# A two-block sequence model in float32 on one core: two re-orderings, in the opening norm and after the last expert

## The chip, the cores and the metric

The program runs on one core of one Trainium2 chip. The metric is the device time of one execution in microseconds; it was measured three times. The core has a matrix engine (TensorE, in the profile PE, with its weight loads as PEld), a vector engine (VectorE, DVE), a scalar engine (ScalarE, ACT), GpSimd (POOL, not used here) and SyncE (SP), whose queue issues all the transfers. The engines run on their own and meet only at semaphores. SBUF is the on-chip memory of 128 partitions; PSUM has eight banks of 512 float32 columns, which TensorE writes.

## The reference

`x` is 512 tokens by 1024. Block 1 is a norm, a projection, two mixers (a gated spatial mixer, and a state space model called S5 here), a merge with a residual, then 16 experts, each of which takes the 64 tokens that score best for it. Block 2 is a norm, a gated recurrence beside a retention, and a convolved FFN. Everything is float32.

```python
h = rms_norm(x, norm1_g[l])
p = h @ w_in[l]
...
gate, idx = lax.top_k(scores, cap)                       # 16 experts, 64 tokens each
a = jnp.einsum('becd,edf->becf', xs, w_gate)
u = jnp.einsum('becd,edf->becf', xs, w_up)
y = jnp.einsum('becf,efd->becd', jax.nn.silu(a) * u, w_down)
y = (y * gate[..., None]).astype(h.dtype)
out = jax.ops.segment_sum(y.reshape(-1, dm), seg, num_segments=bn * seq)
...
return rms_norm(x, final_g)                              # end of block 1, start of block 2
```

## The kernel before

Outside the experts a product of float32 values is made of three products of a faster type (fp32r). A weight chunk of 1 MB lands in `raw`; ScalarE rounds it into `hi` (`make_hi`, line 408), VectorE takes the rest, `lo = raw - hi` (`make_lo`, line 417); the activations are split in the same way into `xh` and `xl`, in eight tiles of 128 x 512 (tile k holds features 128k to 128k+127 of all tokens). TensorE adds hi by xh, hi by xl and lo by xh (line 471). The experts' products are plain float32. The order of work on each engine is the order in which the code is written, since each takes its instructions in turn. Chunks are numbered; `hi_done`, `lo_done` and `pe_used` count those rounded, subtracted and used up.

**Opening.** `first_act` and `first_dve` split x (`x_hi`, line 748, and `rest`, line 904), with `x_in0` to `x_in2` telling that tiles 0-1, 2-3 and 4-7 have landed. Chunk 0 has 256 columns and is used tile by tile (lines 635 to 637), so TensorE waits for `xl` of each tile. Between these splits stand small operations for the S5 tables in `TY` (16 columns each): two Sin on ScalarE (lines 763, 764), whose function table must be loaded first, and after them, on VectorE, products of `TY` (lines 921 to 931), the start values `BB` and `BF`, and powers `PW`, `PT`, `PD` (to line 959). Then `inputs(q)` and `outputs(q)`, for four quarters q, make `V` and `CL` by six wide operations each (lines 873 to 881), which TensorE takes in `tables(q)` (lines 608, 620). The squares of x (`sq`, line 514) are summed on TensorE (line 531), ScalarE takes the root (line 549), VectorE the reciprocal (line 991, `rb_done`), and TensorE spreads it (`spread_first`: lines 542 and 646) in the middle of chunk 1, after output tile 1 of 4 of its hi pass. `take` (line 987) multiplies a pair of chunks' result in PSUM by the spread `rb`; its `qq_taken` frees PSUM for the next pair.

**Experts.** A stream of 192 chunks of 2 MB (`load_x`), 12 for each expert, runs through a ring of eight buffers `xs`: eight chunks of gate and up weights (line 1231) and four of down weights (`down`, line 1243). A down chunk holds 512 of the 2048 rows of `w_down` by all 1024 columns, so the output `ps[:, YB]` is complete only after the fourth. Its matmuls have 64 columns of weights (64 tokens in `hidT`) and write one half of the partitions each: columns 0 to 511 of the result to partitions 0 to 63, the others to 64 to 127. ScalarE then copies the result times the gate value into `yy` (line 1350), TensorE spreads `yy` over the tokens with the one-hot matrix `t1` (`scatter`, line 588, eight matmuls, one for each tile of x), and VectorE adds each to `xt` (`take_scattered`, line 1420). Experts go in pairs, and the scatter of a pair stands in the next pair; that of the last pair stands behind everything.

**Start of block 2.** ScalarE makes `xh` (line 1698) and two squares (line 1700) of each tile of `xt`, VectorE `xl` (line 1466). The first chunk of block 2 (`NEXP`, which is 21) is used tile by tile; the sums of the squares (line 1485) follow it, then chunk 22. Its buffers `hi[0]` and `lo[0]` lie where `xs[2]` lay.

## Time and profile before

| | us |
|---|---|
| median of three runs | 1861.78 (1859.52 to 1862.80) |
| profiled execution, its own time | 1860.12 |
| its span | 1858.4 |
| PE busy | 1714.5 (92%) |
| DVE busy / ACT busy | 658.4 / 445.4 |
| DMA moved | 492.52 MB |

The profiled execution's own time is 1.7 us above its span and 1.7 us below the median of the three runs. Times in the rows are counted from the start of the span. PE busy is not PE at its peak, since matmuls overlap; an idle time is shown in brackets with what ended it. The granted clock is given as a share of full speed: 1.00 is 2.4 GHz, 0.50 is 1.2 GHz.

### The profile page before, as it was taken

The numbers are of one execution on the slowest core, as the hardware profiler recorded it, in microseconds if no ns is written. First come the engines' busy times: TensorE is split into PE (matmuls) and PEld (weight loads), VectorE is DVE, ScalarE is ACT, GpSimd is POOL, SyncE is SP. The second block draws the span as 40 slices with busy tenths as digits, with TensorE's granted clock in tenths as the row PEclk, the third lists the DMA queues.
The fourth block names the chain that finished last, engine by engine and source line by source line (L and its number), as shares of the span: only waits on it lengthen the run. The fifth ranks groups of instructions, "written<-read, shape, count | busy, mean of one in ns | idle before, by whom it ended". The sixth has DMA issues, their size and how long they took to land. (4 is left out here: it accounts for less than half of the span.)

```text
span 1858.4 us, 20146 instructions
## 1 busy us (share of the span) xinstructions
PE 1714.5 (92%) x8461; PEld 1036.3 (56%) x8461; DVE 658.4 (35%) x916; ACT 445.4 (24%) x555; POOL 0.2 (0%) x4
## 2 busy tenths in 40 slices
PE   6999996999897997988979889789999999999998
PEld 5888883343242432424324243247778888888886
DVE  8786533101010010100101001047645565645745
ACT  5434322110010100101001010055433433423333
POOL 0000000000000000000000000000000000000000
PEclk9999998999999999999999999999999999999999
DMA  6234437999999999999999999952412223222311
GB/s 201 69 104 160 164 146 278 409 428 428 427 428 427 428 429 429 428 428 428 428 428 429 428 428 428 428 207 89 158 67 70 91 91 113 90 92 90 113 46 45
DMA packets 74920, 492.52 MB, mean 265 GB/s; under 512 B 7408, under 2 KB 11504, under 8 KB 49904
## 3 DMA queue, kind: packets, MB, share of 16 engines
q1 hardware_dynamic: 74864, 491.71, 65.5%
q8 instruction: 43, 0.70, 0.2%
q14 instruction: 13, 0.11, 0.0%
HBM read 487.49 MB, written 2.10 MB: 263 GB/s over the span
## 5 line engine op out<-in xcount | busy, mean ns | idle before, releaser
L1231 PE MATMUL ps<-xs,xe 128*64 128x512 f32 x2048 | 462.9, 600 | 66.0 <-DMA xs<-w_up 33.1
L1231 PEld LDWEIGHTS ps<-xs,xe 128*64 128x64 f32 x2048 | 142.2, 137 | 379.5 <-issue 265.8
L1243 PE MATMUL ps<-xs,hidT 128*64 128x512 f32 x1024 | 229.7, 596 | 14.1 <-DMA xs<-w_down 9.9
L417 DVE TENSOR_TENSOR lo<-raw,hi 128x2048 fp32r<-128x2048 f32 x72 | 162.6, 2259 | 170.2 <-ACT hi L408 167.2
L1452 DVE TENSOR_TENSOR hid<-hid,ps 128x512 f32<-128x512 f32 x32 | 20.6, 684 | 525.9 <-PE ps L1231 525.9
L408 ACT ACTIVATE hi<-raw 128x2048 fp32r<-128x2048 f32 x72 | 136.0, 1889 | 204.5 <-PE ps L447 93.9
L471 PE MATMUL ps<-xh,hi 128*128 128x512 f32 x416 | 164.9, 396 | 0.9 <-DVE ga L987 0.9
L471 PE MATMUL ps<-xl,hi 128*128 128x512 f32 x416 | 162.3, 390 | 0.0
L1243 PEld LDWEIGHTS ps<-xs,hidT 128*64 128x64 f32 x1024 | 73.7, 137 | 148.3 <-issue 120.5
L447 PE MATMUL ps<-xh,hi 128*128 128x512 f32 x384 | 150.2, 391 | 1.4 <-DVE xt L2013 1.1
L447 PE MATMUL ps<-xl,hi 128*128 128x512 f32 x384 | 149.4, 389 | 0.0
L471 PE MATMUL ps<-xh,lo 128*128 128x512 f32 x416 | 102.1, 390 | 0.0
L447 PE MATMUL ps<-xh,lo 128*128 128x512 f32 x384 | 90.9, 389 | 0.0
L471 PEld LDWEIGHTS ps<-xh,hi 128*128 128x128 f32 x416 | 78.1, 188 | 20.0 <-issue 2.6
L471 PEld LDWEIGHTS ps<-xl,hi 128*128 128x128 f32 x416 | 78.1, 188 | 15.9 <-issue 0.2
L471 PEld LDWEIGHTS ps<-xh,lo 128*128 128x128 f32 x416 | 77.8, 188 | 16.2
L1338 ACT ACTIVATE hidT<-ps 128x512 f32<-128x512 f32 x32 | 18.6, 597 | 281.5 <-PE ps L1271 281.5
L447 PEld LDWEIGHTS ps<-xh,hi 128*128 128x128 f32 x384 | 72.0, 188 | 18.1 <-issue 3.0
L1420 DVE TENSOR_TENSOR xt<-xt,ps 128x512 f32<-128x512 f32 x64 | 44.0, 688 | 107.6 <-PE ps L588 107.6
L1335 ACT ACTIVATE hid<-ps 128x512 f32<-128x512 f32 x32 | 17.4, 594 | 267.2 <-PE ps L1231 267.1
L447 PEld LDWEIGHTS ps<-xl,hi 128*128 128x128 f32 x384 | 72.1, 188 | 15.1 <-issue 0.2
L447 PEld LDWEIGHTS ps<-xh,lo 128*128 128x128 f32 x384 | 72.1, 188 | 15.0
(432 smaller groups left out, 1747.5 us busy)
## 6 DMA issues: line engine op xcount, KB each, us to landing
xs<-w_up SPq DMA_DIRECT2D x64, 2048.0 KB, 32.8
xs<-w_gate SPq DMA_DIRECT2D x64, 2048.0 KB, 31.9
xs<-w_down SPq DMA_DIRECT2D x64, 2048.0 KB, 31.4
raw<-w_in SPq DMA_DIRECT2D x24, 1024.0 KB, 7.7
raw<-ffn_up_w SPq DMA_DIRECT2D x24, 1024.0 KB, 5.1
raw<-ffn_down_w SPq DMA_DIRECT2D x12, 1024.0 KB, 5.1
raw<-w_out SPq DMA_DIRECT2D x8, 1024.0 KB, 5.1
raw<-w_up_a SPq DMA_DIRECT2D x2, 1024.0 KB, 7.6
```

What stands on the lines that cost most here:

```text
L408: act.activation(hi[slot][:, 0:size], raw[:, raw_slot(n), 0:size], ACT.Copy).then_inc(sem("hi_done"), 1)
L417: dve.tensor_tensor(lo[slot][:, 0:size], raw[:, raw_slot(n), 0:size], hi[slot][:, 0:size].bitcast(F32), ALU.subtract).then_inc(sem("lo_don ...
L447: mm = pe.matmul(ps[:, bank + m, 0:nn if token_major else SEQ], l, r, start=(k == 0 and part == 0 and q == 0), stop=(last and part == 1 an ...
L471: mm = pe.matmul(ps[:, bank + m, :], l, r, start=(opens and kk == 0 and part == 0 and q == 0), stop=(closes and part == 1 and kk == nk - 1))
L1231: mm = pe.matmul(ps[64 * half:64 * half + 64, bank + b, :], xe[:, k, CAP * u:CAP * (u + 1)], xs[n % NXS][:, f:f + 512], start=(k == 0), st ...
L1243: mm = pe.matmul(ps[64 * nn:64 * nn + 64, YB, :], hidT[:, 4 * (c % 2) + kk, CAP * half:CAP * (half + 1)], xs[n % NXS][:, kk * D + nn * 512 ...
L1335: a(hid[:, 512 * b:512 * b + 512], ps[:, GB + b, :], ACT.Silu).then_inc(sem("sil_done"), 1)
L1338: a(hidT[:, 4 * b:4 * b + 4, :].rearrange("p k c -> p (k c)"), ps[:, TB + b, :], ACT.Copy) \
L1420: tt(xt[:, m, :], xt[:, m, :], ps[:, TB + m % 3, :], ALU.add).then_inc(sem("sc_taken"), 1)
L1452: tt(hid[:, 512 * b:512 * b + 512], hid[:, 512 * b:512 * b + 512], ps[:, UB + b, :], ALU.mult) \
```

## The change

There are two parts.

In the opening, ScalarE makes `xh` of tiles 4 to 7 before the two Sin, VectorE makes `xl` of tiles 4 to 7 before the products of `TY`, and the reciprocal moves ahead of chunk 1's `make_lo` and of `inputs(0)`.

After the experts, the last expert's down weights arrive in another cut: chunk q holds all 2048 rows of columns 256q to 256q+255, from a copy `w_down_q` that the host lays out, so a quarter of the result is complete after each chunk. Chunk q takes 32 matmuls of 128 columns in place of 8 of 512. The third quarter lies in the second halves of `xs[6]` and `xs[7]`, the fourth in `xq3`, over space that the gathered tokens used; The space of `xh` and `xl` of tiles 0 to 3 (the first halves of the same two buffers) is not used by these chunks. SyncE issues the third quarter after 184 used chunks and not 183. After each quarter ScalarE evicts two pieces of 64 x 128, and TensorE scatters the two tiles of the quarter before; VectorE adds tiles 0 to 5 before chunk 21's `make_lo` and tiles 6 and 7 after it.

```diff
@@ first_act
             x_hi(range(2, 4))
+            x_hi(range(4, KD))
             a(TY[:, 10, :], TY[:, 6, :], ACT.Sin).then_inc(sem("exp_done"), 1)
             a(TY[:, 11, :], TY[:, 7, :], ACT.Sin).then_inc(sem("exp_done"), 1)
-            x_hi(range(4, KD))
@@ first_dve
-            for k in range(2, 4):
+            for k in range(2, KD):
                 rest(k)
...
+            dve.wait_ge(sem("nrm_rms"), 1)
+            dve.reciprocal(rs[0], rs[0]).then_inc(sem("rb_done"), 1)
             make_lo(dve, 1)
...
             inputs(0)
-            dve.wait_ge(sem("nrm_rms"), 1)
-            dve.reciprocal(rs[0], rs[0]).then_inc(sem("rb_done"), 1)
             make_lo(dve, 2)
@@ experts_pe
+            def down_by_columns(i):
+
+                pe.wait_ge(sem("hidT_done"), i * 4 + 4)
+                for q in range(4):
+                    n = NX - 4 + q
+                    x_arrived(pe, n, 0)
+                    if q >= 2:
+                        pe.wait_ge(sem("yy_done"), YLAST + 2 * (q - 1))
+                    home = last_home[q]
+                    for c in range(4):
+                        for kk in range(4):
+                            f = 256 * (4 * c + kk)
+                            for nn in range(2):
...
+                                mm = pe.matmul(ps[64 * nn:64 * nn + 64, last_bank(q), 0:P],
+                                               hidT[:, 4 * (c % 2) + kk, CAP * (c // 2):CAP * (c // 2 + 1)], wv,
+                                               start=(c == 0 and kk == 0), stop=(c == 3 and kk == 3))
+                    mm.then_inc(sem("xs_used"), 1)
+                    if q:
+                        last_scatter(q - 1)
+                last_scatter(3)
+
+            def last_scatter(q):
+
+                if q == 0:
+                    pe.wait_ge(sem("t1_done"), NE // 2 + 1)
+                pe.wait_ge(sem("yy_done"), YLAST + 2 * (q + 1))
+                for m in (2 * q, 2 * q + 1):
+                    if m >= 2:
+                        pe.wait_ge(sem("sc_taken"), KD * (NE // 2) + min(m, 6))
+                    pe.matmul(ps[:, scatter_bank(m), :], yy[:, m * P:(m + 1) * P], t1[:], start=True, stop=True) \
+                        .then_inc(sem("sc_ps"), 1)
@@ experts_act
-                        act.wait_ge(sem("xs_used"), NX - 4)
+                        for q in range(4):
+                            act.wait_ge(sem("xs_used"), NX - 3 + q)
+                            for nn in range(2):
+                                o = 64 * nn
+                                a(yy[64:P, 256 * q + 128 * nn:256 * q + 128 * nn + 128], ps[o:o + 64, last_bank(q), 0:P], ACT.Copy,
+                                  scale=cur[o:o + 64, 1, 1:2]).then_inc(sem("yy_done"), 1)
+                            if 1 <= q < 3:
+                                new_tile(act, 2 * q - 2)
+                                new_tile(act, 2 * q - 1)
                         make_hi(act, NEXP)
+                        break
@@ experts_dve
-            make_lo(dve, NEXP)
...
+            for m in range(4):
+                add_last(m)
+                if m % 2:
+                    new_rest(m - 1)
+                    new_rest(m)
+            for m in range(4, KD):
+                if m == 6:
+                    make_lo(dve, NEXP)
+                add_last(m)
+            for m in range(4, KD):
+                new_rest(m)
             make_lo(dve, NEXP + 1)
@@ second_act (new_tile is the old loop's body: xh and two squares)
+            for m in range(4, KD):
+                new_tile(act, m)
+                if m == 5:
                     make_hi(act, NEXP + 1)
@@ sync
+            for q in range(4):
+                n = NX - 4 + q
+                sp.wait_ge(sem("xs_used"), min(n - NXS + 1, NX - NXS) if q < 2 else NX - NXS)
+                src = w["w_down_q"][:, q, :]
+                d(last_home[q], src.rearrange("p (a b) -> p a b", a=2) if q == 2 else src).then_inc(x_sem(n % NXS), 16)
```

On VectorE, the place of the reciprocal. `lo_54` is chunk 1's rest, `V` is made by `inputs(0)`, `sm` is the norm's reciprocal. Before:

```order
L958 COPY PD<-PW 64x256
L959 COPY PD<-PW 64x256
L417 TENSOR_TENSOR lo_54<-raw,hi_51 128x2048
L873 TENSOR_TENSOR V_67<-PD,BB 128x512
L874 TENSOR_TENSOR TMP<-PD,BB 128x512
L875 TENSOR_TENSOR V_67<-PD,BB 128x512
L876 TENSOR_TENSOR TMP<-PD,BB 128x512
L877 TENSOR_TENSOR V_67<-V_67,TMP 128x512
L881 TENSOR_TENSOR V_67<-V_67,TMP 128x512
L991 RECIPROCAL sm<-sm 128x128
```

And in the changed kernel, where the same lines have numbers higher by 3 to 5:

```order
L961 COPY PD<-PW 64x256
L962 COPY PD<-PW 64x256
L964 RECIPROCAL sm<-sm 128x128
L422 TENSOR_TENSOR lo_54<-raw,hi_51 128x2048
L878 TENSOR_TENSOR V_67<-PD,BB 128x512
L879 TENSOR_TENSOR TMP<-PD,BB 128x512
L880 TENSOR_TENSOR V_67<-PD,BB 128x512
L881 TENSOR_TENSOR TMP<-PD,BB 128x512
L882 TENSOR_TENSOR V_67<-V_67,TMP 128x512
L886 TENSOR_TENSOR V_67<-V_67,TMP 128x512
L422 TENSOR_TENSOR lo_53<-raw,hi_50 128x2048
```

The reciprocal now stands in front of seven operations that it stood behind.

On ScalarE, the place of the Sin table. Before:

```order
L748 ACTIVATE xh<-xin,prm 128x512 x2
L763 ACT_TABLE_LOAD
L763 ACTIVATE TY<-TY 128x16
L764 ACTIVATE TY<-TY 128x16
L748 ACTIVATE xh<-xin,prm 128x512 x4
L514 ACTIVATE sq<-xin 128x512 x8
```

Now:

```order
L753 ACTIVATE xh<-xin,prm 128x512 x6
L769 ACT_TABLE_LOAD
L769 ACTIVATE TY<-TY 128x16
L770 ACTIVATE TY<-TY 128x16
L519 ACTIVATE sq<-xin 128x512 x8
```

The four `xh` operations moved in front of the table load and the two Sin.

On TensorE, the last expert's down chunks, the scatter (`t_135` is the one-hot matrix) and the first matmul of block 2. Before:

```order
L1243 MATMUL ps<-xs_140,hidT 64x512 x8
L1243 MATMUL ps<-xs_141,hidT 64x512 x8
L1243 MATMUL ps<-xs_142,hidT 64x512 x8
L1243 MATMUL ps<-xs_143,hidT 64x512 x8
L588 MATMUL ps<-t_135,yy 128x512 x8
L471 MATMUL ps<-xh,hi_50 128x512
```

Now:

```order
L1317 MATMUL ps<-xs_140,hidT 64x128 x32
L1317 MATMUL ps<-xs_141,hidT 64x128 x32
L1333 MATMUL ps<-t_135,yy 128x512 x2
L1317 MATMUL ps<-x_144,hidT 64x128 x32
L1333 MATMUL ps<-t_135,yy 128x512 x2
L1317 MATMUL ps<-xq_145,hidT 64x128 x32
L1333 MATMUL ps<-t_135,yy 128x512 x4
L476 MATMUL ps<-xh,hi_50 128x512
```

Each quarter has 32 matmuls where a chunk had 8, and the scatter's eight stand two, two and four.

## Rows read from the trace of the kernel before

**Rows 1.** Windows by stage: PE, PEld, DVE, ACT, POOL busy, clock, DMA share, GB/s.
```profile
340.00:1222.00 882.00, 789.45 (x3640) 297.51 (x3636) 73.94 (x140) 72.91 (x148) 0.00 (x0) 1.00 1.01 428
...
1236.00:1376.00 140.00, 138.16 (x639) 107.42 (x638) 90.08 (x85) 67.59 (x71) 0.00 (x0) 1.00 0.27 96
```

**Rows 2.** Timeline of TensorE: start, us, what; its waits in the first stage.
```profile
17.40 0.36 PE L635 MATMUL ps<-hi,xh 128*128 128x256 f32 x1 [0.77 <-DVE xl L904]
...
34.97 0.81 PE L542 MATMUL ps<-sm 32*128 32x128 f32 x8 [5.80 <-DVE sm L991]
...
139.57 0.50 PE L471 MATMUL ps<-xh,hi 128*128 128x512 f32 x1 [0.85 <-DVE ga L987]
```

**Rows 3.** Busy time by stretch around the wait at 29 us; clock after POOL.
```profile
29.10:35.00 5.90, 0.10 (x5) 0.03 (x4) 5.83 (x9) 0.00 (x0) 0.00 (x0) 0.81 0.54 178
35.00:39.60 4.60, 4.60 (x18) 3.60 (x19) 4.60 (x5) 2.12 (x6) 0.00 (x0) 0.50 0.27 60
```

**Rows 4.** Timeline of VectorE, 14 to 36 us.
```profile
14.39 0.18 DVE L921 TENSOR_TENSOR TY<-TY 128x16 f32<-128x16 f32 x1 [0.83 <-ACT TY L764]
...
19.31 1.05 DVE L940 MEMSET BF<- 128x528 f32 x2
...
27.90 2.29 DVE L417 TENSOR_TENSOR lo<-raw,hi 128x2048 fp32r<-128x2048 f32 x1
...
33.96 0.95 DVE L991 RECIPROCAL sm<-sm 128x128 f32<-128x128 f32 x1
```

**Rows 5.** Timeline of ScalarE, 12 to 17 us.
```profile
12.75 1.28 ACT L763 ACT_TABLE_LOAD   x1
...
14.27 2.55 ACT L748 ACTIVATE xh<-xin,prm 128x512 fp32r<-128x512 f32 x4
16.72 4.26 ACT L514 ACTIVATE sq<-xin 128x512 f32<-128x512 f32 x8
```

**Rows 6.** Issue of x's last four tiles on SyncE's queue.
```profile
3.07 0.83 SPq L2169 DMA_DIRECT2D xin<-x_t  x1
```

**Rows 7.** DMA issues, 0 to 80 us: count, KB, us to landing.
```profile
xin<-x_t SPq DMA_DIRECT2D x1, 1024.0 KB, 10.9
```

**Rows 8.** Timeline of VectorE: its waits before table products and gates.
```profile
56.92 0.69 DVE L873 TENSOR_TENSOR V<-PD,BB 128x512 f32<-128x512 f32 x1 [4.98 <-PE ps L608]
...
83.75 2.48 DVE L987 TENSOR_TENSOR ga<-ps,rb 128x512 f32<-128x512 f32 x4 [1.81 <-PE ps L471]
```

**Rows 9.** Timeline of TensorE: last expert's down products, first chunk.
```profile
1207.78 3.65 PE L1243 MATMUL ps<-xs,hidT 128*64 128x512 f32 x16
```

**Rows 10.** Timeline of TensorE: third and fourth chunk.
```profile
1216.54 3.65 PE L1243 MATMUL ps<-xs,hidT 128*64 128x512 f32 x16 [1.15 <-DMA xs<-w_down]
...
1222.17 3.65 PE L1243 MATMUL ps<-xs,hidT 128*64 128x512 f32 x16 [1.98 <-DMA xs<-w_down]
```

**Rows 11.** Source line 701: 64 instructions of 128x64 weights by 128 columns.
```profile
L701 PEld LDWEIGHTS ps<-wsT,vg x64: 137/137/137, 166.7 to 170.4; 128*64 128x64 f32 x64
L701 PE MATMUL ps<-wsT,vg x64: 272/272/273, 166.8 to 170.5; 128*64 128x128 f32 x64
```

**Rows 12.** Timeline after the last down chunk, all engines.
```profile
1224.93 1.91 ACT L408 ACTIVATE hi<-raw 128x2048 fp32r<-128x2048 f32 x1 [16.65 <-DMA raw<-w_in]
1226.87 1.39 ACT L1350 ACTIVATE yy<-ps,cur 64x512 f32<-64x512 f32 x2
...
1228.31 7.13 PE L588 MATMUL ps<-t,yy 128*128 128x512 f32 x16 [2.48 <-ACT yy L1350]
...
1229.47 0.69 DVE L1420 TENSOR_TENSOR xt<-xt,ps 128x512 f32<-128x512 f32 x1 [0.31 <-PE ps L588]
...
1230.19 0.72 ACT L1698 ACTIVATE xh<-xt,sm 128x512 fp32r<-128x512 f32 x1 [1.94 <-DVE xt L1420]
...
1235.26 0.47 PE L471 MATMUL ps<-xh,hi 128*128 128x512 f32 x1
```

**Rows 13.** Timeline of ScalarE: hidT of the last expert.
```profile
1207.09 1.20 ACT L1338 ACTIVATE hidT<-ps 128x512 f32<-128x512 f32 x2 [18.18 <-PE ps L1271]
```

More of the change, by code:

```diff
@@ L110, in lay_out @@
         "w_s": i["w_in"][0][:, 1024:1024 + SW].reshape(KD, P, SW).transpose(1, 0, 2),
+        "w_down_q": i["w_down"][0][NE - 1].reshape(4, P, 4, 4, 256).transpose(1, 3, 0, 2, 4).reshape(P, 4, XCH),
         "gmlp_ws_t": i["gmlp_w_s"][0].transpose(2, 0, 1),
@@ L290, in build @@
         xs = [at(f"xs{j}", [P, XCH], F32, (0, 16, 32, 48, 102, 118, 64, 80)[j]) for j in range(NXS)]
+        x67 = at("x67", [P, 2, XCH], F32, 64)
+        xq3 = at("xq3", [P, XCH], F32, B + 73)
+        last_home = (xs[4][:], xs[5][:], x67[:, :, XCH // 2:], xq3[:])
         kr = at("kr", [P, RH, SEQ], F32, B)
@@ L934, in gh @@
                 return v.unsqueeze(2).to_broadcast([P, SG, SH])
-            for k in range(4, KD):
-                rest(k)
             dve.wait_ge(sem("s5_in"), 32)
@@ L1209, in rest_of_indices, with last_bank, scatter_bank @@
             mm.then_inc(sem("idb_ps"), 1)
+        YLAST = 4 * (NE // 2 - 1) + 3
+        def last_bank(q):
+            return (YB, TB + 2)[q % 2]
+        def scatter_bank(m):
+            return (TB + m % 2, YB, TB)[max(m - 5, 0)]
         def experts_pe(pe):
@@ L1273, in pair @@
                     pe.wait_ge(sem("yy_done"), i * 4 + (2 * u + 1))
+                    if u == 1 and last:
+                        down_by_columns(i)
+                        break
                     for c in range(4):
@@ L1284, in pair @@
                                 gather(pe, k)
+            def down_by_columns(i):
[10 more added lines that the diff above has]
+                            for nn in range(2):
+                                wv = home[:, f // 2048, f % 2048 + 128 * nn:f % 2048 + 128 * nn + 128] if q == 2 else \
+                                    home[:, f + 128 * nn:f + 128 * nn + 128]
+                                mm = pe.matmul(ps[64 * nn:64 * nn + 64, last_bank(q), 0:P],
[14 more added lines that the diff above has]
+                        .then_inc(sem("sc_ps"), 1)
             pair(0, first=True)
@@ L1289, in experts_pe @@
             pair(NE // 2 - 1, last=True)
-            for q in range(4):
-                scatter(pe, NE // 2, q)
         def experts_act(act, a):
@@ L1457, in experts_dve, with new_rest, add_last, new_tile @@
             pair(NE // 2 - 1, last=True)
-            make_lo(dve, NEXP)
             stt = dve.scalar_tensor_tensor
-            for m in range(KD + 5):
-                if m < KD:
-                    take_scattered(m, KD * (NE // 2) + m + 1)
-                k = m - 5
-                if k >= 0:
-                    dve.wait_ge(sem("xh_done"), KD + k + 1)
-                    stt(xl[:, k, :], xt[:, k, :], gxx[:, k:k + 1], xh[:, k, :].bitcast(F32), ALU.mult, ALU.subtract) \
-                        .then_inc(sem("xl_done"), 1)
+            def new_rest(m):
+                dve.wait_ge(sem("xh_done"), KD + m + 1)
+                stt(xl[:, m, :], xt[:, m, :], gxx[:, m:m + 1], xh[:, m, :].bitcast(F32), ALU.mult, ALU.subtract) \
+                    .then_inc(sem("xl_done"), 1)
+            def add_last(m):
+                dve.wait_ge(sem("sc_ps"), KD * (NE // 2) + m + 1)
+                tt(xt[:, m, :], xt[:, m, :], ps[:, scatter_bank(m), :], ALU.add).then_inc(sem("sc_taken"), 1)
+            for m in range(4):
[9 more added lines that the diff above has]
+                new_rest(m)
             make_lo(dve, NEXP + 1)
         N2, SCS = NEXP, 1 + KD * (NE // 2 + 1)
+        def new_tile(act, m):
+            act.wait_ge(sem("sc_taken"), SCS - KD + m + 1)
+            act.activation(xh[:, m, :], xt[:, m, :], ACT.Copy, scale=gxx[:, m:m + 1]).then_inc(sem("xh_done"), 1)
+            for j, g in enumerate((None, gss)):
+                act.activation(squared(j, m), xt[:, m, :], ACT.Square, scale=1.0 if g is None else g[:, m:m + 1]) \
+                    .then_inc(sem("nrm_sq"), 1)
         def squared(j, k):
@@ L1692, in second_act @@
         def second_act(act, a):
-            for m in range(KD):
-                if m == 4:
+            for m in range(4, KD):
+                new_tile(act, m)
+                if m == 5:
                     make_hi(act, NEXP + 1)
-                act.wait_ge(sem("sc_taken"), SCS - KD + m + 1)
-                a(xh[:, m, :], xt[:, m, :], ACT.Copy, scale=gxx[:, m:m + 1]).then_inc(sem("xh_done"), 1)
-                for j, g in enumerate((None, gss)):
-                    a(squared(j, m), xt[:, m, :], ACT.Square, scale=1.0 if g is None else g[:, m:m + 1]) \
-                        .then_inc(sem("nrm_sq"), 1)
             make_hi(act, N2 + 2)
@@ L2235, in _ @@
                     load_x(n, i)
-            for n in range(NX - 16, NX):
+            for n in range(NX - 16, NX - 4):
                 load_x(n)
+            for q in range(4):
[3 more added lines that the diff above has]
+                d(last_home[q], src.rearrange("p (a b) -> p a b", a=2) if q == 2 else src).then_inc(x_sem(n % NXS), 16)
             for j in range(4):
```

7 lines of the change are left out of this document (4 added, 3 removed).

## The prediction

> **What bounds the kernel now.** I read the busy time by stage first. From 340 to 1222 us the DMA share is 1.01 at 428 GB/s while TensorE has idle gaps, so the experts are bound by the weight stream: 2.1 MB each 4.9 us. Behind them, from 1236 to 1376 us, TensorE is busy 138.2 of 140.0 us [rows 1]. So a gain must come from what stands before the stream or from the hand-over behind it, and it must hold TensorE's path there. I read next TensorE's waits in the first stage. There are three of note: 0.77 us at 17.4 for `xl`, 5.80 us at 29.2 for the reciprocal, 0.85 us at 139.6 for a `take` [rows 2]. Then the windows around the second: the clock is 0.50 (1.2 GHz) from 35.0 to 39.6 us, after an idle stretch in which it fell [rows 3]. Last the end of the experts: TensorE ends the last down chunk at 1222.17 + 3.65 = 1225.8 and starts block 2 at 1235.26, 9.4 us later, after an idle 2.48 and eight scatter matmuls of 7.13 us together [rows 10, 12].
>
> **The opening: what the reciprocal waits for.** VectorE ends the powers and starts chunk 1's `make_lo` at 27.90 (2.29 us), then makes six products, and only at 33.96 the reciprocal (0.95 us), at whose end, 34.9, TensorE goes on [rows 2, 4]. Placed in front, it would start at 27.9 and end at 28.85 if nothing else moved. But the splits of x move too. Tiles 4 to 7 of x are issued at 3.07 and take 10.9 us, so they land at 13.97 [rows 6, 7]. ScalarE would be ready for them at 12.75, and now waits idle until 13.97; then come four `xh` (2.55 us, to 16.5), the table load of 1.28 and the two Sin. Before, the load began at 12.75 and VectorE began its table products at 14.39, 1.64 later [rows 4, 5]. Now that is 16.5 + 1.64 = 18.15. The products took 2.1 us (14.39 to the next splits, which came before 19.31), so the memset that stood at 19.31 stands at about 20.3: VectorE is 1.0 us later, its four `xl` having been done by 17.5 in the meantime. The reciprocal starts at 28.9 and ends at 29.85.
>
> TensorE itself loses the 0.77 us wait, since `xl` of tile 4 is there at 15.5. The squares start at 18.0 and not 16.72, take 4.26 us and end at 22.2, about when TensorE ends chunk 0, so it gets to the spread at about 28.2 and waits there some 1.6 us in place of 5.80. The spread starts at 29.9 in place of 34.97: **5.1 us**. So the 0.77 us are worth nothing by themselves; they become part of the shorter wait.
>
> The clock comes on top. In the 4.6 us from 35.0 to 39.6 TensorE did at 0.50 what it does in 2.3 us at 1.00 [rows 3]. It waited 1.98 us for a transfer at the end of the experts without a slower matmul behind it (3.65 us, as the chunk after the 1.15 us wait) [rows 10], so a wait of 1.6 us should leave the clock at 1.00: **2.3 us** more. TensorE's lead is then 7.4 us.
>
> **What of it is kept.** VectorE has no lead of its own; it is 1.0 us late until it first waited for TensorE, at 56.92 for 4.98 us. There its lead becomes 4.98 - 1.0 = 4.0, less than TensorE's 7.4, but nothing of TensorE's is late yet: `outputs(2)`, which takes the next table, is wanted only two chunks later. The next wait, 1.81 us before the first `take` at 83.75, brings it to 5.9 (with 0.15 us of a small wait between) [rows 8]. Now the `take` is late: TensorE, 7.4 early, has its bank freed 0.45 us after it wants it, which leaves 6.95. The last place is the `take` at 139.57, on which TensorE waited already [rows 2]: VectorE reaches it 5.9 early, some 0.2 us after TensorE's product is ready. That leaves **6.7 us**. Between ends: 4.0 if the table products bind after all, 7.6 if the squares and the Sin cost VectorE nothing. After this the routing and the stream's first issues all hang on TensorE's and VectorE's last products of the stage, so the whole stream begins 6.7 us earlier and has the same bytes.
>
> **The hand-over, in the times of before.** The first quarter needs both halves of `hidT`, ready at 1207.09 + 1.20 = 1208.3, where the old first chunk began at 1207.78 [rows 9, 13]. The price of a quarter: 64 instructions of 128x64 weights by 128 columns. Line 701 has exactly 64 of this form, with output in the two halves of the partitions as here, and they start from 166.8 to 170.5, which makes 3.75 us [rows 11]. A scatter matmul is 7.13 / 8 = 0.88 us, two are 1.75 [rows 12]. TensorE now does quarter, quarter, two scatters, quarter, two scatters, quarter: 4 x 3.75 + 2 x 1.75 = 18.5 us, so the last quarter ends at **1226.8**. The chunks land at about 1211.7, 1216.5 and 1222.2, each 0.3 to 0.8 us before TensorE wants it now; TensorE has become the later one by a little, and the last quarter ends 1.0 us later than the old last chunk.
>
> From there: tiles 4 and 5 are scattered; in the kernel before the first add began 1.16 us after the first scatter [rows 12], so the adds of 4 and 5 run from 1228.0 to 1229.6. ScalarE evicts the last two pieces; 64 x 128 has no row, the two of 64 x 512 took 1.39 us [rows 12], and I take 0.6 between nothing and that. Its `make_hi` of 1.91 us then ends at 1229.3, with `raw` landed at 1224.93 as before [rows 12]. VectorE's `make_lo` starts at 1229.6 and takes 2.29 [rows 4]: TensorE starts block 2 at **1231.9** in place of 1235.26. That is **3.4 us**. With evictions of 1.39 us it is 2.7; with quarters at the streaming pace it could be 4.5. Hidden work: the scatter and adds of tiles 0 to 3, and `xh`, the squares and `xl` of these tiles, lie beside the third and fourth quarter; each ScalarE tile is three operations of 0.72 at most [rows 12], two tiles fit into one quarter's 5.5 us, and without that cover up to half a microsecond would delay the last eviction. Behind the `make_lo` wait the adds of 6 and 7 and `xl` 4 to 7; they are wanted after chunk 21's 11 us, and take about 8.
>
> **Sum.** 6.7 + 3.4 = 10.1 us. Against the profiled execution's 1860.12: 1850.0. The median of the three runs is 1.66 above that execution, so I forecast **1851.7**.
>
> **Rival 1, VectorE takes the first gain back.** It stays at its 4.0 us lead because a table product binds. For it: these are its only long waits until then [rows 8]. Against: the first wait shows 4.98 us in hand. Result 4.0 - 0.2 + 3.4 = 7.2: 1854.6. Chance 0.10.
>
> **Rival 2, the quarters land late.** The third is issued one used chunk later, and all read columns out of another copy. Each microsecond of the last landing beyond 0.8 costs one; at 4.2 us the hand-over's gain is gone: 1855.1. Against: eight buffers at 4.9 us each leave some seven chunks queued in front of it. Chance 0.07.
>
> **Rival 3, the stream does not start earlier,** so that 6.7 us turn into waits for transfers, and only the 3.4 are left: 1858.4. For it: the DMA share of 1.01 [rows 1]. Against: the queue is filled only after the first stage's last products. Chance 0.05.
>
> **Rival 4, slower: weight loads stop hiding.** With 128 columns a matmul pair streams for a quarter of the time, and each still needs its loads (137 ns each) [rows 11]. If loads were not hidden, a pair would cost 0.14 + 0.11 us and a quarter of 32 pairs 7.9 us. TensorE's path to the last quarter's end grows by 4 x (7.9 - 3.75) = 16.6 us: 10.1 gained less 16.6 is 6.5 lost, 1868.3. It decides from a quarter of 3.75 + 10.1 / 4 = 6.3 us on. Against: line 701 did 64 of them in 3.75 us with loads of 137 ns, so they were hidden there [rows 11]. Chance 0.06.
>
> Here the Trainium skill speaks against the change: its page TensorE: Matmul & The Clock Gate, section The mechanism, says that weight loads overlap with running matmuls only when the row group differs, and all of a quarter's share their rows. By that rule rival 4 holds, and the sum is 1868.3. The trace disagrees: 64 loads of 137 ns would alone fill 8.8 us one behind the other, and the whole took 3.75 [rows 11].
>
> **How the numbers follow.** The forecast holds 0.72, with 1849 to 1854 by the ends of its own terms and the spread of the runs. Rivals 1 and 2 reach to 1855, with their own spread to 1857. The range 1848.5 to 1857 leaves out rivals 3 and 4 and a little of each tail. About 0.2% (3.7 us) is what a measurement here can tell from no change, so rivals 1 and 2 still count as faster: 0.89. Within it lies rival 3, 0.05; slower is rival 4, 0.06.
>
> **What would show it.** The reciprocal stands before chunk 1's `lo`, ends near 29.9, and TensorE's wait there is 1 to 2 us with a clock of 1.00 from 24 to 60 us. ScalarE idles 1.2 us before the fifth `xh`. At 139 us the same product stands near 133, and the stream ends near 1215. In the hand-over a group of 64 instructions of 128x128 takes 3.7 to 3.9 us, and the first matmul of block 2 follows the last of them by about 5.1 us. A quarter above 4.5 us, a clock of 0.50 after the shorter wait, or a wait for `w_down_q` above 1 us before the last quarter would make the prediction wrong.

## The result, and the profile after

| | before | changed |
|---|---|---|
| median of six runs, same chip, in turn | 1861.31 us (1858.57 to 1862.95) | 1851.85 us (1849.52 to 1852.87) |
| profiled execution, its own time | 1860.12 | 1852.32 |
| its span | 1858.4 | 1850.5 |
| PE busy | 1714.5 | 1714.0 |

The ratio is 0.995, with a 95% interval of 0.994 to 0.996. The forecast was 1851.7 us, a sum of 10.1; the medians lie 9.5 apart. TensorE is busy as long as before, so what went away is nearly all waiting: the slow clock that the opening lost is nearly made up by one that this profile has later, at `kr` (below).

The opening, in the timeline of VectorE, where the rows answer to [rows 4]:

```profile
14.83 2.74 DVE L909 SCALAR_TENSOR_TENSOR xl<-xin,prm,xh 128x512 fp32r<-128x512 f32 x4 [0.91 <-ACT xh L753]
18.31 0.18 DVE L926 TENSOR_TENSOR TY<-TY 128x16 f32<-128x16 f32 x1 [0.73 <-ACT TY L770]
...
29.15 0.95 DVE L964 RECIPROCAL sm<-sm 128x128 f32<-128x128 f32 x1
30.02 2.23 DVE L422 TENSOR_TENSOR lo<-raw,hi 128x2048 fp32r<-128x2048 f32 x1
```

The same stretch of ScalarE, to be read against [rows 5]:

```profile
14.07 2.56 ACT L753 ACTIVATE xh<-xin,prm 128x512 fp32r<-128x512 f32 x4 [1.22 <-DMA xin<-x_t]
16.66 1.28 ACT L769 ACT_TABLE_LOAD   x1
```

TensorE's two waits of the first stage that are left, against [rows 2]:

```profile
30.16 0.50 PE L547 MATMUL ps<-sm 32*128 32x128 f32 x8 [0.52 <-DVE sm L964]
...
132.93 0.50 PE L476 MATMUL ps<-xh,hi 128*128 128x512 f32 x1 [0.96 <-DVE ga L992]
```

And the busy time of one stretch (length, then PE, PEld, DVE, ACT, POOL, granted clock, DMA share, GB/s). Over the same 36 us the kernel before had a PE of 30.20 and a clock of 0.91.

```profile
24.00:60.00 36.00, 35.48 (x265) 29.16 (x258) 34.91 (x68) 16.26 (x21) 0.00 (x0) 1.00 0.38 103
```

The 5.80 us wait is 0.52, the eight spread matmuls take 0.50 us and not 0.81, and the clock stays at 1.00, the 2.4 GHz level. The matmul that waits for the `take`, at 139.57 before, starts at 132.93: 6.64 us are kept.

The hand-over, in the timeline of TensorE, against [rows 9, 10, 12]:

```profile
1202.24 7.21 PE L1317 MATMUL ps<-xs,hidT 128*64 128x128 f32 x128 [0.73 <-issue]
1209.38 1.98 PE L1333 MATMUL ps<-t,yy 128*128 128x512 f32 x4
1211.30 3.71 PE L1317 MATMUL ps<-x,hidT 128*64 128x128 f32 x64
1214.94 1.98 PE L1333 MATMUL ps<-t,yy 128*128 128x512 f32 x4
1216.86 3.71 PE L1317 MATMUL ps<-xq,hidT 128*64 128x128 f32 x64
1220.50 3.95 PE L1333 MATMUL ps<-t,yy 128*128 128x512 f32 x8
1225.73 0.47 PE L476 MATMUL ps<-xh,hi 128*128 128x512 f32 x1 [1.28 <-issue]
```

A quarter is one group of 64: each of its 32 float32 matmuls stands in the profile as two instructions, and each of the eight of the scatter too. The first row holds two quarters. Nothing here waits for a transfer. The two engines that meet TensorE at the end, in their own timelines, ScalarE first:

```profile
1220.62 0.75 ACT L1396 ACTIVATE yy<-ps,cur 64x128 f32<-64x128 f32 x2 [0.19 <-PE ps L1317]
1221.39 1.91 ACT L413 ACTIVATE hi<-raw 128x2048 fp32r<-128x2048 f32 x1
```

VectorE, the same stretch:

```profile
1221.66 0.69 DVE L1526 TENSOR_TENSOR xt<-xt,ps 128x512 f32<-128x512 f32 x1 [1.58 <-PE ps L1333]
1222.52 0.69 DVE L1526 TENSOR_TENSOR xt<-xt,ps 128x512 f32<-128x512 f32 x1 [0.17 <-PE ps L1333]
1223.33 2.29 DVE L422 TENSOR_TENSOR lo<-raw,hi 128x2048 fp32r<-128x2048 f32 x1
```

The last quarter ends at 1220.5, its evictions and `make_hi` at 1223.3, `make_lo` at 1225.6, and block 2 starts. From the last quarter's end to block 2 are 5.2 us, where the old last chunk needed 9.4.

Block 2 starts 9.53 us earlier (1235.26 to 1225.73), but the span is only 7.9 shorter. The difference lies behind one wait for `kr`, 1.85 us long in this profile, 1.84 in the one before. The changed kernel, TensorE's timeline and the window behind it:

```profile
1337.49 3.80 PE L1599 MATMUL ps<-qr,kr 128*128 128x512 f32 x8 [1.85 <-DVE kr L2016]
...
1337.50:1341.00 3.50, 3.50 (x9) 2.17 (x9) 2.29 (x1) 0.16 (x1) 0.00 (x0) 0.62 0.00 0
```

And the kernel before:

```profile
1347.05 2.42 PE L1520 MATMUL ps<-qr,kr 128*128 128x512 f32 x8 [1.84 <-DVE kr L1941]
...
1347.05:1350.50 3.45, 3.45 (x14) 2.44 (x15) 3.21 (x3) 0.16 (x1) 0.00 (x0) 1.00 0.00 0
```

The same eight matmuls take 3.80 us at a clock of 0.62 and 2.42 at 1.00. The change touches neither them nor the wait. Eleven more profiles, below, show that it goes with neither part of the change.

### The profile page after: what moved, and what is told of

Read it like the earlier page. It is cut to its first block and busy times, and to the rows that moved or that the text cites. A ratio compares the mean times of both kernels' runs of the same rounds, so it can differ in the third digit from the quotient of the medians.

```text
span 1850.5 us, 20537 instructions
## 1 busy us (share of the span) xinstructions
PE 1714.0 (93%) x8653; PEld 1045.3 (56%) x8653; DVE 658.1 (36%) x916; ACT 447.3 (24%) x561; POOL 0.2 (0%) x4
## 5 line engine op out<-in xcount | busy, mean ns | idle before, releaser
L1256 PE MATMUL ps<-xs,hidT 128*64 128x512 f32 x960 | 215.0, 596 | 10.7 <-DMA xs<-w_down 6.6
L1256 PEld LDWEIGHTS ps<-xs,hidT 128*64 128x64 f32 x960 | 68.8, 137 | 135.9 <-issue 112.7
L1383 ACT ACTIVATE hid<-ps 128x512 f32<-128x512 f32 x32 | 17.4, 594 | 265.0 <-PE ps L1244 265.0
L1477 DVE TENSOR_TENSOR xt<-xt,ps 128x512 f32<-128x512 f32 x56 | 38.5, 688 | 106.4 <-PE ps L593 106.4
```

The source lines that it names most:

```text
L1256: mm = pe.matmul(ps[64 * nn:64 * nn + 64, YB, :], hidT[:, 4 * (c % 2) + kk, CAP * half:CAP * (half + 1)], xs[n % NXS][:, kk * D + nn * 512 ...
L1383: a(hid[:, 512 * b:512 * b + 512], ps[:, GB + b, :], ACT.Silu).then_inc(sem("sil_done"), 1)
L1477: tt(xt[:, m, :], xt[:, m, :], ps[:, TB + m % 3, :], ALU.add).then_inc(sem("sc_taken"), 1)
```

## The experiments

Every kernel was timed in turn with the kernel before on one chip, and profiled once; each ratio is against the kernel before in the same series. All edits are made to the kernel before or to the changed kernel, as said. Three starts of rows are read in each profile, all in TensorE's timeline, and their differences tell the parts apart:

- **router**: the router's matmuls that wait 0.2 us for `xt`, where the first stage ends (279.71 before);
- **down**: the eight transposes ahead of the last expert's down weights (1206.30 before);
- **block 2**: its first matmul (1235.26 before).

| kernel | router | down | block 2 less down | block 2 | `kr` matmuls | ratio, 95% interval |
|---|---|---|---|---|---|---|
| before | 279.71 | 1206.30 | 28.96 | 1235.26 | 2.42 | |
| changed | 273.05 | 1200.16 | 25.57 | 1225.73 | 3.80 | 0.9950 (0.994 to 0.996) |
| opening_only | 272.93 | 1200.17 | 28.93 | 1229.10 | 2.42 | 0.9968 (0.9955 to 0.998) |
| tail_only | 278.56 | 1204.47 | 25.56 | 1230.03 | 2.42 | 0.9983 (0.9974 to 0.9992) |
| recip_only | 271.81 | 1198.77 | 31.56 | 1230.33 | 2.42 | 0.9967 (0.9955 to 0.9979) |
| splits_only | 280.77 | 1207.46 | 30.44 | 1237.90 | 2.42 | 1.0004 (0.9995 to 1.0013) |
| recip_mid | 273.73 | 1200.97 | 28.95 | 1229.92 | 4.09 | 0.9970 (0.9959 to 0.9981) |
| first_quarter_twice | 272.19 | 1198.71 | 29.05 | 1227.76 | 2.42 | 0.9967 (0.9954 to 0.9979) |
| split_before_adds | 272.63 | 1199.14 | 28.96 | 1228.10 | 2.42 | 0.9969 (0.9956 to 0.9981) |
| scatters_at_end | 273.14 | 1200.04 | 33.90 | 1233.94 | 2.42 | 0.9997 (0.9988 to 1.0007) |
| order_only | 280.01 | 1206.60 | 31.46 | 1238.06 | 4.03 | 1.0015 (1.0006 to 1.0024) |
| recip_and_tail | 273.09 | 1199.68 | 25.56 | 1225.24 | 4.12 | 0.9932 (0.9918 to 0.9945) |
| hidt_order | 273.59 | 1200.16 | 25.35 | 1225.51 | 4.04 | 0.9944 (0.9931 to 0.9958) |

### The two parts, each alone

`opening_only` has the opening's three moves and the old tail; `tail_only` has the old opening and the new tail.

```diff
@@ opening_only, on the kernel before
+            x_hi(range(4, KD))
             a(TY[:, 10, :], TY[:, 6, :], ACT.Sin).then_inc(sem("exp_done"), 1)
             a(TY[:, 11, :], TY[:, 7, :], ACT.Sin).then_inc(sem("exp_done"), 1)
-            x_hi(range(4, KD))
...
-            for k in range(2, 4):
+            for k in range(2, KD):
                 rest(k)
...
-            for k in range(4, KD):
-                rest(k)
...
+            dve.wait_ge(sem("nrm_rms"), 1)
+            dve.reciprocal(rs[0], rs[0]).then_inc(sem("rb_done"), 1)
             make_lo(dve, 1)
...
             inputs(0)
-            dve.wait_ge(sem("nrm_rms"), 1)
-            dve.reciprocal(rs[0], rs[0]).then_inc(sem("rb_done"), 1)
```

`tail_only` is the changed kernel with the same lines undone.

> The kernel before with the opening's part alone (reciprocal ahead of chunk 1's split and of the table products, splits of x ahead of the Sin). Theory: the two parts add, and this one is worth 6.7 us by the forecast's sum, kept through the stream: ratio 0.9964, start of block 2 some 6.1 to 6.7 us before 1235.26. Rival (the stream takes the gain back, and all of the measured 9.5 us comes from the hand-over): no change.

> The changed kernel with the opening as before. Theory: the quarters and the adds are worth 3.4 us: ratio 0.9982, and from the transposes of the last expert to the first matmul of block 2 25.6 us in place of 29.0. Rival (the stream takes the opening's gain back): the whole 9.5 us, ratio 0.995.

`opening_only`: 1854.12 us. The router comes 6.78 us earlier and the old hand-over is unchanged, 28.93. `tail_only`: 1857.54 us, a hand-over of 25.56, thus 3.40 us shorter. In both the part that was not made stays away, and the product of the two ratios is 0.9951 against 0.9950 measured. The two parts add up, as the sum in the prediction assumed. The stream does not take the opening's gain back, and neither profile has the loss at `kr`.

### The opening taken apart

`recip_only` is the kernel before with the reciprocal's move alone, `splits_only` with the moves of `x_hi` and `rest` alone, the other lines of the diff above:

```diff
@@ recip_only, on the kernel before
+            dve.wait_ge(sem("nrm_rms"), 1)
+            dve.reciprocal(rs[0], rs[0]).then_inc(sem("rb_done"), 1)
             make_lo(dve, 1)
...
             inputs(0)
-            dve.wait_ge(sem("nrm_rms"), 1)
-            dve.reciprocal(rs[0], rs[0]).then_inc(sem("rb_done"), 1)
```

> The kernel before with only the reciprocal moved, the splits of x behind the Sin as they were. Theory: VectorE is then not 1.0 us late, the reciprocal runs from 27.9 to 28.85, TensorE comes at 29.2 after its 0.77 us wait for the fifth tile and waits no more; VectorE leads by 5.0 at the first table product and 6.8 at the first gate, so 7.6 to 7.7 us are kept at 139 us: 0.9 us better than with the splits moved too, ratio 0.9959. Rival (the splits are what pays, the wait at 17.4 being the first on TensorE's path): worse than with both, by 0.8 us or more.

> The kernel before with only the splits of x moved ahead of the Sin. Theory: the wait of 0.77 us at 17.4 goes, and VectorE is 1.0 to 1.2 us later at the reciprocal, so the spread starts at 36 in place of 34.97 and TensorE is 1.0 us later there: ratio 1.0005, slower by 0.5 to 1.2 us. Rival: the 0.77 us is a gain of its own, ratio 0.9996.

The reciprocal carries the gain by itself: TensorE's timeline of `recip_only` has the spread with no wait ahead of it, and VectorE's has the reciprocal where the second split stood [rows 4]:

```profile
29.11 0.50 PE L542 MATMUL ps<-sm 32*128 32x128 f32 x8
...
27.90 0.95 DVE L961 RECIPROCAL sm<-sm 128x128 f32<-128x128 f32 x1
```

Its router comes 7.9 us earlier, as expected, but the median is 1854.7, where a ratio of 0.9959 was expected: it is not to be told from `opening_only`, so the 0.9 us by which it should be better do not show in the time. Its 31.56 in the tail are worth a look, since the code there is the old one. Two rows of its timeline make up the 2.6 us:

```profile
1210.57 3.65 PE L1243 MATMUL ps<-xs,hidT 128*64 128x512 f32 x16 [2.71 <-DMA xs<-w_down]
...
1221.68 8.83 PE L588 MATMUL ps<-t,yy 128*128 128x512 f32 x16 [2.47 <-ACT yy L1350]
...
1221.70:1230.30 8.60, 8.60 (x16) 3.53 (x17) 5.74 (x9) 6.51 (x12) 0.00 (x0) 0.80 0.05 19
```

A transfer came late (0.9 us of it are left after the fourth chunk), and the scatter behind the 2.47 us wait took 8.83 us at a clock of 0.80 where it took 7.13 before [rows 12]. Neither comes from the edit: `order_only`, whose stream is the same, also has its third chunk late, behind a wait of 2.38 us, and `splits_only` has a slow scatter too (8.65 us).

The moved splits alone earn nothing: 1861.75 us, and in the profile the spread starts at 35.51 behind a wait of 6.25, against 34.97 and 5.80 [rows 2]. That is 0.54 us later, in the direction that the working gave (VectorE 1.0 late), but the three profiles with the old opening (`before`, `tail_only`, `order_only`) lie from 34.58 to 35.42 themselves, and the ratio does not tell it from nothing either.

In `recip_mid` the reciprocal stands behind the split and ahead of `inputs(0)`.

```diff
@@ recip_mid, on the kernel before
             make_lo(dve, 1)
+            dve.wait_ge(sem("nrm_rms"), 1)
+            dve.reciprocal(rs[0], rs[0]).then_inc(sem("rb_done"), 1)
             inputs(0)
```

> The kernel before with the reciprocal behind chunk 1's split and ahead of the table products. Theory: it runs from 30.1 to 31.05, TensorE waits 1.9 us, the clock stays at 1.00, and the lead is 3.9 us of wait and 2.3 of clock, 6.2; VectorE's lead limits it: 5.0 at 56.9, 6.8 at the first gate, so 6.0 to 6.2 are kept: ratio 0.9967. Rival (the clock falls in any wait of this length): about 4 us, ratio 0.9979.

TensorE's timeline of `recip_mid`, and the window from 24 to 60 us:

```profile
31.11 0.50 PE L542 MATMUL ps<-sm 32*128 32x128 f32 x8 [1.73 <-DVE sm L962]
...
24.00:60.00 36.00, 34.27 (x252) 28.10 (x244) 34.98 (x63) 14.84 (x20) 0.00 (x0) 1.00 0.38 103
```

A wait of 1.73 us is left and the clock keeps to 1.00, as the prediction had taken it for a wait of 1.6. The router is 6.0 us earlier. Here the clock's share shows apart from the wait's: 4.07 us of wait are gone (5.80 to 1.73), and 1.9 more are kept. (Counted from the spread's start, which is 3.86 us earlier, it is 2.1.) The median is 1856.19; its profile lost 1.6 us at `kr` again. Another stretch of it speaks against the reason that the prediction gave for the clock; see the part on why it was right.

### The hand-over taken apart

`first_quarter_twice` issues the first quarter's 64 instructions a second time, over the first: extra work, with the same output.

```diff
@@ first_quarter_twice, on the changed kernel
-                    for c in range(4):
+                    for c in [c for _ in range(2 if q == 0 else 1) for c in range(4)]:
```

> The changed kernel with the first quarter's 32 matmuls done twice (the second time over the first's result, so nothing else changes). Theory: from the first quarter on TensorE is the bound, so block 2 starts later by the whole of one quarter, 3.6 to 3.75 us (the line in the trace: from the last expert's transposes to block 2 29.2 us in place of 25.6). Rival (the landings are the bound and TensorE has time in hand): 1 us or less.

TensorE's timeline of it, the first quarter's two passes and the second quarter in one group:

```profile
1200.79 10.70 PE L1317 MATMUL ps<-xs,hidT 128*64 128x128 f32 x192 [0.73 <-issue]
```

Block 2 comes 29.05 us after the transposes, 3.48 more than in the changed kernel, for 3.5 us more of TensorE. So TensorE's own work is what bounds this stretch, not the landings, and a quarter's price is charged in full. The median is 1854.13 us, 6.4 below the kernel before in its series, where the changed kernel was 9.5 below.

`split_before_adds` has chunk 21's `make_lo` ahead of the adds of tiles 4 and 5.

```diff
@@ split_before_adds, on the changed kernel
-                if m == 6:
+                if m == 4:
                     make_lo(dve, NEXP)
```

> The changed kernel with VectorE's split of chunk 21 ahead of the adds of tiles 4 and 5. Theory: TensorE's last two scatters wait for a bank that the add of tile 4 frees, and stand ahead of block 2 on TensorE, so they now wait for the split as well: split from 1223.3 to 1225.6 in the changed kernel's times, add of tile 4 to 1226.3, two scatters to 1228.1: block 2 starts 2.3 us later than 1225.73. Rival (the split is the last thing that block 2 waits for, so doing it first pays): 0.5 us earlier or no change.

TensorE's timeline, then two windows of the same kernel ahead of and behind its wait:

```profile
1219.48 1.98 PE L1333 MATMUL ps<-t,yy 128*128 128x512 f32 x4
1225.34 3.75 PE L1333 MATMUL ps<-t,yy 128*128 128x512 f32 x4 [3.88 <-DVE xt L1526]
...
1219.48:1221.50 2.02, 1.98 (x6) 0.67 (x4) 0.00 (x0) 1.86 (x3) 0.00 (x0) 1.00 1.02 375
1225.30:1233.00 7.70, 7.66 (x19) 4.83 (x20) 3.95 (x6) 7.70 (x12) 0.00 (x0) 0.65 0.19 70
```

The loss at block 2's start is 3.39 us, 1.1 more than expected. VectorE's split, now in front, holds up the adds, the adds hold the PSUM banks, and the last two scatters wait 3.88 us. Behind the wait they take 3.75 us and not 1.98, at half the clock, and block 2's first matmuls go on so: from its start to the `kr` wait it takes 113.30 us and not 111.76, another 1.5 us. The missing 1.1 lies in those 1.8 us of slow scatters.

`scatters_at_end` has all scatters behind the four quarters.

```diff
@@ scatters_at_end, on the changed kernel
-                    if q:
-                        last_scatter(q - 1)
-                last_scatter(3)
+                for q in range(4):
+                    last_scatter(q)
```

> The changed kernel with all eight scatters behind the fourth quarter, the other engines' order unchanged. Theory: the cover of the third and fourth quarter is lost: the last quarter ends 0.8 us earlier, but ScalarE's tiles 0 to 3 and VectorE's first adds and xl stand in front of the last evictions and of chunk 21's splits, so block 2 starts 8 to 9 us later: ratio 0.9995 against the kernel before. Rival (the scatters' place is of no matter, the quarters themselves pay): within 1.5 us of the changed kernel.

Its timeline of TensorE shows new waits behind the second quarter; these are the first three of five:

```profile
1210.35 3.71 PE L1317 MATMUL ps<-x,hidT 128*64 128x128 f32 x64 [1.02 <-DMA x<-w_down_q]
1215.28 3.71 PE L1317 MATMUL ps<-xq,hidT 128*64 128x128 f32 x64 [1.22 <-DMA xq<-w_down_q]
1218.93 3.95 PE L1332 MATMUL ps<-t,yy 128*128 128x512 f32 x8
1225.23 3.52 PE L1332 MATMUL ps<-t,yy 128*128 128x512 f32 x4 [2.36 <-ACT yy L1395]
```

Block 2 comes 8.3 us later than in the changed kernel, and with 1860.6 us the whole gain of both parts is gone. The last quarter ends at 1218.9, 1.5 us sooner after the transposes, but from there to block 2 are 15.0 us and not 5.2. Two things make this up. The scatters no longer fill the time in which the next quarter lands, and TensorE does them behind everything. And ScalarE, whose order was left as it is, makes the new tiles 0 and 1 ahead of the third quarter's eviction, and these tiles now wait for the scatters; the waits of 2.36 and 0.88 us for `yy` come from this, and so does the longer one ahead of block 2, 2.33 us. So the early quarters pay only with scatters that are issued at once, in this order of ScalarE; the scatters at the end with the evictions first were not run.

`order_only` has the adds of six tiles ahead of chunk 21's `make_lo`, and the down weights by rows as before.

```diff
@@ order_only, on the kernel before
-            make_lo(dve, NEXP)
             stt = dve.scalar_tensor_tensor
             for m in range(KD + 5):
+                if m == 6:
+                    make_lo(dve, NEXP)
```

> The kernel before with chunk 21's VectorE split behind six adds, and the down weights by rows as before. Theory: the order alone costs, since all adds wait for the scatters behind the fourth chunk: six adds end at 1234.5, the first xl follows, the split ends at 1237.5, and block 2 starts about 2.2 us later than 1235.26: ratio 1.0012. Rival (the order is what pays and the quarters only make room): faster by 1 us or more.

Its timeline of TensorE, the scatter and block 2's first matmul:

```profile
1228.95 7.13 PE L588 MATMUL ps<-t,yy 128*128 128x512 f32 x16 [2.47 <-ACT yy L1350]
1238.06 0.47 PE L471 MATMUL ps<-xh,hi 128*128 128x512 f32 x1 [1.97 <-DVE lo L417]
```

The order of adds and split without the quarters loses 2.50 us: 0.34 ahead of the scatter, in the stream, and the rest behind it, where the wait for `lo` in the second row stands. The kernel is slower, 1864.53 us, with the whole interval above 1. In the old tail `lo` was done before the adds began; put behind them it is the last thing that TensorE waits for. The order pays only with the quarters, which have six of the eight adds done before the split could start; with them, the other order lost 3.39 us (`split_before_adds`).

### Two versions that go further

`recip_and_tail` is the changed kernel with the splits of x back in their old place, on both engines. In `hidt_order` the down quarters also take the rows of `hidT`'s first half first.

```diff
@@ recip_and_tail, on the changed kernel (first_act; rest(k) in first_dve likewise)
-            x_hi(range(4, KD))
             a(TY[:, 10, :], TY[:, 6, :], ACT.Sin).then_inc(sem("exp_done"), 1)
             a(TY[:, 11, :], TY[:, 7, :], ACT.Sin).then_inc(sem("exp_done"), 1)
+            x_hi(range(4, KD))
@@ hidt_order, on recip_and_tail
-                pe.wait_ge(sem("hidT_done"), i * 4 + 4)
+                pe.wait_ge(sem("hidT_done"), i * 4 + 3)
...
-                    for c in range(4):
+                    for c in (0, 2, 1, 3):
+                        if q == 0 and c == 1:
+                            pe.wait_ge(sem("hidT_done"), i * 4 + 4)
```

> The changed kernel without its moved splits of x: reciprocal first, quarters and adds as changed. Theory: the traces of the parts show TensorE 1.1 us further ahead at 272 us without the moved splits, and the parts add: 7.8 + 3.4 = 11.2 us in the trace's stages, ratio 0.994 to 0.9945, as fast as the changed kernel or up to 1 us faster. Rival (the moved splits pay, as the median of the run without them, 0.6 us above the one with them, would have it): 0.5 us or more slower than the changed kernel's 0.995.

> As recip_and_tail, and in each quarter the rows are summed in the order 0, 2, 1, 3, so that the first half of the first quarter needs only the first half of hidT. Theory: TensorE is the bound from the first quarter on, so starting it 0.5 to 0.6 us earlier brings everything behind it 0.5 us forward: 0.5 us less than recip_and_tail. Rival (landings bound the quarters): no difference.

`recip_and_tail` has the lowest median of all, 1849.52 us (1847.79 to 1851.72). Its interval, 0.9918 to 0.9945, overlaps the changed kernel's, 0.994 to 0.996, so it beats the kernel before, and the changed one perhaps. It is faster than was expected of it (0.994 to 0.9945). `hidt_order` takes 0.21 us off the hand-over where 0.5 was expected; its second quarter now waits for its landing, in its timeline of TensorE:

```profile
1201.64 3.71 PE L1321 MATMUL ps<-xs,hidT 128*64 128x128 f32 x64
1205.52 3.71 PE L1321 MATMUL ps<-xs,hidT 128*64 128x128 f32 x64 [0.16 <-DMA xs<-w_down_q]
```

TensorE starts 0.6 us sooner after the transposes (the 0.73 us wait is gone) and runs into the stream. Its median, 1852.08 us, is above that of `recip_and_tail` and not below; the intervals overlap, so the runs show no gain.

## Why the prediction was right

It was right in the total and in every large term. What was off is small, and one reason, that for the clock, was weaker than it looked.

- **The reciprocal's place.** Forecast start 28.9, measured 29.15; spread forecast 29.9, measured 30.16. The chain of causes held: ScalarE idles 1.22 us, the splits go first, the table load starts at 16.66 (16.5).
- **What is left of the wait.** Forecast 1.6 us, measured 0.52. TensorE came later, not the reciprocal sooner: in this profile its first matmul started at 10.64, against 9.38 before, as x's first tiles landed later. The spread follows the reciprocal, which was 1.25 us later than in `recip_only` and not 1.0, and so the spread gained 4.81 and not 5.1.
- **The clock's 2.3 us.** The window from 24 to 60 us is at 1.00, and in each of the nine profiles in which the wait was 1.73 us or less (five of them have none). `recip_mid` shows it at a wait like the one forecast. The reason given was a single row, 1.98 us of waiting with no slow matmul behind it, and that row does not carry it. The same profile has a wait of 2.26 us for a transfer, 40 us earlier, with a slow clock behind it: 0.58 in the next 4 us, and two chunks, 32 instructions, in 8.78 us, where two at full speed take 7.3:

```profile
1182.43 8.78 PE L1231 MATMUL ps<-xs,xe 128*64 128x512 f32 x32 [2.26 <-DMA xs<-w_gate]
```

  And `recip_mid` has at 1212.01 the same slow 8.78 us, at a clock of 0.57 to begin with, behind a wait of 1.95 us, less than the 1.98. That the clock kept to 1.00 here was therefore likely, not sure, and the wait came out at 0.52.
- **The 1.0 us that VectorE was charged for the splits.** It is there. ScalarE idles 1.15 to 1.22 us before the fifth `xh` in all six profiles with moved splits, and VectorE's memset of `BF` starts 6.5 us after this `xh`, as it starts 6.6 us after the table load where the splits stand in their old place: VectorE is 1.1 us late. From the reciprocal's start (29.15 in the changed kernel, 27.90 in `recip_only`) to the router it takes 243.87 to 243.91 us in six of the eight profiles with the reciprocal in front of chunk 1's split, so a microsecond of VectorE there is a microsecond at the router. In the other two, `recip_and_tail` and `hidt_order`, it takes 244.55 and 245.19: there TensorE was the later one, its first matmul having started at 10.48 and 10.81, and VectorE waits 0.59 and 0.84 us at the last `take`. This hides the charge in a mean over these eight: the router starts on average at 272.79 in the five with moved splits and at 272.83 in the three without.
- **The 0.77 us at 17.4.** The prediction held it to be worth nothing by itself. Of the seven profiles with the splits in their old place only that of the kernel before shows this wait at all, so the moved splits cost VectorE 1.1 us and had mostly nothing to remove. Whether the time is better without them stays open: `recip_and_tail` has the lower median, `recip_only` not.
- **What is kept.** Forecast 6.7 at 139 us, measured 6.64. The step as told, that VectorE reaches this `take` 5.9 early and loses the wait it had, is to be read in VectorE's own rows. Before, then the changed kernel:

```profile
138.82 2.48 DVE L987 TENSOR_TENSOR ga<-ps,rb 128x512 f32<-128x512 f32 x4 [0.84 <-PE ps L471]
```

```profile
132.19 2.48 DVE L992 TENSOR_TENSOR ga<-ps,rb 128x512 f32<-128x512 f32 x4
```

  VectorE was ready for it at 137.98 before and is at 132.19 now, 5.8 earlier, and the 0.84 us for which it waited are gone. On the way it was 3.8 us early at the first table product (53.11; forecast 4.0) and 5.7 at the first gate (78.05; forecast 5.9). Rival 1, VectorE stopping at 4.0, fell with this.
- **The stream starts earlier.** From the router to the last expert's transposes it takes 927.1 us against 926.6; 0.5 of the 6.66 us were lost on the way, where `opening_only` and `first_quarter_twice` lost 0.6 and nothing (927.2 and 926.5); over all thirteen profiles it is 925.9 to 927.2, so this is variation. Rival 3 is out. The quarters' landings: no wait in the changed kernel, and in `hidt_order` the second is 0.16 us late once TensorE comes sooner, so TensorE is the later one by little, as forecast; in `scatters_at_end`, where TensorE meets the third and the fourth, they are there 0.8 and 1.5 us before the changed kernel wants them. Rival 2 is out.
- **The quarter.** Forecast 3.75 us, measured 3.71, and 3.6 for each of the two in a row. Its weight loads, by line:

```profile
L1317 PEld LDWEIGHTS ps<-xq,hidT x64: 133/137/137, 1216.9 to 1220.2; 128*64 128x64 f32 x64
L1317 PE MATMUL ps<-xq,hidT x64: 272/273/323, 1216.9 to 1220.3; 128*64 128x128 f32 x64
```

  64 loads of 137 ns are 8.8 us, and all of them start within 3.3: they are hidden, and as recorded they overlap each other. Rival 4 fell. The Trainium skill (page TensorE: Matmul & The Clock Gate, section The mechanism) has it that a load overlaps only where the row group differs, and all 64 have the same rows and two halves of the output columns; as a rule for this case that does not hold, and the measurement decides. The same section of the Trainium skill also lets a load run ahead into the background weight buffer, which the prediction did not weigh; which way these loads were hidden no run shows.
- **The hand-over.** Forecast 3.4, measured 3.39, and 25.56 to 25.57 in all three kernels that have this tail (the changed one, `tail_only`, `recip_and_tail`). The evictions took 0.75 us where 0.6 was taken between bounds of 0 and 1.39, the last adds lay beside `make_hi` as told, and from the last quarter's end to block 2 it took 5.2 us (5.1).
- **The sum.** 6.66 at the router, less 0.52 in the stream, and 3.39 make 9.53 at block 2, against 10.1. The profiled execution then lost 1.6 us at `kr` and came out at 7.8 less than its counterpart, while the medians came out 9.5 apart. That forecast and median differ by only 0.15 us is luck in part: the gain was 0.6 us less than forecast, and the median before, 1861.78 when the forecast was made, was 1861.31 this time. The medians' own range is 3 us.

## What to carry to other kernels

Look for a short operation on which the busiest engine waits and which stands behind wide ones that nobody needs yet; its wait may also cost the clock behind it, so the gain is more than the wait. Where a sum over a long stream must be complete before the next step can start, cut the weights so that a part of the result is complete after each transfer, but issue what uses that part at once: with the scatters at the end the gain was gone (`scatters_at_end`, though with an order of ScalarE that was made for early scatters), and the new order of adds and split lost time without the cut (`order_only`). When a change's profile shows less than its medians, compare the distance between landmarks that the change does not touch before looking for a cause in the change.

## What the runs showed of the hardware

- **After a wait of about 2 us the clock falls in some profiles and not in others.** Behind the same wait of 1.84 to 1.85 us for `kr` it fell towards the lower level (1.2 GHz) in 5 of 13 profiles: those eight matmuls took 3.80, 4.12, 4.04, 4.09 and 4.03 us, against 2.42 in the other eight, and the way from there to the matmuls on `sw` and `v` that wait 0.61 us for `sw` (1369.09 in the changed kernel) was 31.6 us and not 29.95. Behind waits of 2.2 to 2.5 us for `yy` the scatter was slow in 2 of 6 profiles with the old tail (8.83 and 8.65 us against 7.13). Behind the waits for a transfer of 1.83 to 2.71 us in the last expert it fell in 5 of 16. Behind 4.8 to 6.3 us the spread was slow in 4 of 4, and behind up to 1.73 us there in 0 of 4 (five more have no wait). The five slow profiles at `kr` have both tails and both openings among them, so it goes with neither; no kernel was profiled twice, so that it changes between executions of one kernel is not shown directly. It fits that the mean clock of single executions of the kernel before lay anywhere from 0.989 to 0.992. The new tail waits 1.28 us and not 2.5 before block 2, so it also takes away one such chance. That was not in the prediction.
- **The first landings differ from run to run.** TensorE's first matmul started between 9.38 and 10.97 us in the thirteen profiles. Profiles with the same opening differ by nearly as much at the end of the first stage (278.56 to 280.01 with the old one, 272.19 to 273.14 with the changed one), and 1.1 us between two variants there is no finding by itself: count from the engine that is the later one, as above from the reciprocal, or see whether the medians have it too.
- **Weight loads of 64 columns hide completely** behind matmuls of 128 columns whose outputs go in turn to the two halves of the partitions: 58 ns (3.71 us in all) for each of the 64 instructions, with loads of 137 ns.
